# Opening of the expert stages with four units ahead of the first down product

## The reference, cut to what matters

```python
def hier_moe(xn, w_group, b_group, w_expert, b_expert, w_gate, w_up, w_down):   # xn = rms_norm(h, ln_ffn)
    g_prob = softmax(xt @ w_group + b_group); g_w, g_idx = top_k(g_prob, 1)      # 4 groups
    e_prob = softmax(of the 8 experts of that group); e_w, e_idx = top_k(e_prob, 2)
    comb = g_w * e_w / sum(e_w);  cw = comb at the chosen experts, 0 elsewhere     # [tokens, 32]
    hid = silu(xt @ w_gate[e]) * (xt @ w_up[e])                                   # all 32 experts
    y = sum over e of (hid * cw[:, e]) @ w_down[e]
```

## Time and profile before

| | |
|---|---|
| median of 3 runs | 4208.21 us (4208.19 to 4209.12) |
| profiled execution | 4201.7 us, span 4199.9 us |
| TensorE matmul busy | 3884.0 us, 92% of the span |
| VectorE busy | 2685.7 us, 64% |
| ScalarE busy | 1813.2 us, 43% |
| GpSimd busy | 1456.4 us, 35% |
| mean TensorE clock granted | 0.922 |
| DMA | 664.37 MB, mean 158 GB/s |

### The profile page before, as it was taken

How to read it: one execution, slowest core, us unless ns; L and a number is a source line. 1 busy time by engine, 2 the same in 40 slices (tenths; PEclk the granted TensorE clock), 3 DMA queues, 4 the chain that set the end, 5 groups by cost and what they waited for, 6 DMA issues and landing times.

```text
span 4199.9 us, 69359 instructions
## 1 busy us (share of the span) xinstructions
PE 3884.0 (92%) x28940; PEld 3543.8 (84%) x28940; DVE 2685.7 (64%) x4863; ACT 1813.2 (43%) x3080; POOL 1456.4 (35%) x842
## 2 busy tenths in 40 slices
PE   7998998989989898979999989989999999999899
PEld 6658997679979867769999859989869998867699
DVE  4446776577777775567777867777657644665543
ACT  3233444334454442234545635444444444432343
POOL 2003443044434430034444423434314444320143
PEclk9759998699989999989999999999969999979899
DMA  5104662156646420027575415657516644210143
GB/s 207 56 16 177 259 263 103 59 192 261 254 167 264 179 95 13 1 106 271 226 271 197 151 51 200 267 211 271 190 53 241 264 168 158 96 41 1 45 168 115
DMA packets 63687, 664.37 MB, mean 158 GB/s; under 512 B 7056, under 2 KB 7568, under 8 KB 7952
## 3 DMA queue, kind: packets, MB, share of 16 engines
q1 hardware_dynamic: 63376, 659.94, 41.8%
HBM read 658.86 MB, written 1.05 MB: 157 GB/s over the span
## 4 chain that ended last, share of the span: by engine, by line
PE 79%; DVE 14%; ACT 4%; issue 1%; POOL 1%; DMA 0%; SPq 0%; DVEq 0%; ACTq 0%; POOLq 0%
PE pb L275 76%; PE pb L282 3%; DVE wp L228 2%; DVE wk L240 2%; DVE wk L228 2%; ACT wp L266 2%; DVE sq L240 1%; DVE ada_acc L240 1%; DVE hT L240 1%; ACT wk L266 1%; DVE sq L228 1%; DVE hx L240 0%; DVE hx L228 0%; POOL sq L228 0%; POOL wp L228 0%
## 5 line engine op out<-in xcount | busy, mean ns | idle before, releaser
L275 PE MATMUL pb<-hx,wp 128*128 128x256 f32 x15744 | 1995.8, 288 | 106.7 <-DVE hx L228 51.8
L275 PEld LDWEIGHTS pb<-hx,wp 128*128 128x128 f32 x15744 | 1956.4, 196 | 128.6 <-issue 106.6
L228 POOL TENSOR_TENSOR wp<-ring,wp 128x512 fp32r<-128x512 f32 (+1 forms) x596 | 1250.3, 2114 | 2005.8 <-ACT wp L266 2005.8
L266 ACT ACTIVATE wp<-ring 128x1024 fp32r<-128x1024 f32 x936 | 941.2, 1046 | 258.1 <-PE pb L275 250.9
L228 DVE TENSOR_TENSOR wp<-ring,wp 128x1024 fp32r<-128x1024 f32 (+1 forms) x670 | 796.8, 1206 | 359.3 <-ACT wp L266 355.3
L275 PE MATMUL pb<-ex,wp 128*128 128x256 f32 x5856 | 756.7, 287 | 19.4 <-DVE ex L228 19.4
L275 PEld LDWEIGHTS pb<-ex,wp 128*128 128x128 f32 x5856 | 728.9, 194 | 20.6 <-issue 18.0
L240 DVE SCALAR_TENSOR_TENSOR ada_acc<-ring,cact,ada_acc 128x384 f32<-128x384 f32 x576 | 529.8, 983 | 60.4 <-ACT ada_acc L266 60.2
L275 PE MATMUL pb<-wk 128*128 128x128 f32 (+8 forms) x3136 | 488.4, 327 | 16.8 <-ACT wk L266 7.7
L275 PEld LDWEIGHTS pb<-wk 128*128 128x128 f32 (+4 forms) x3136 | 339.8, 190 | 160.3 <-issue 96.6
L228 DVE TENSOR_TENSOR sq<-sq,pb 128x256 f32<-128x256 f32 (+1 forms) x360 | 161.4, 448 | 323.6 <-ACT sq L266 276.3
(11 more groups left out here) (179 smaller groups left out, 2821.2 us busy)
## 6 DMA issues: line engine op xcount, KB each, us to landing
ring<-weights SPq DMA_DIRECT2D x385, 1536.0 KB, 6.7
ring<-weights SPq DMA_DIRECT2D x41, 1024.0 KB, 4.8
ring<-weights SPq DMA_DIRECT2D x4, 512.0 KB, 10.2
cst<-consts SPq DMA_DIRECT2D x1, 2032.0 KB, 11.8
ring<-weights SPq DMA_DIRECT2D x1, 1280.0 KB, 5.5
prm<-params SPq DMA_DIRECT2D x1, 1258.0 KB, 7.4
ring<-weights SPq DMA_DIRECT2D x1, 1152.0 KB, 4.9
xT<-xT_in SPq DMA_DIRECT2D x1, 1024.0 KB, 4.8
```

Of the source, the lines that this page charges most:

```text
L228: return self.real.tensor_tensor(out, a, b, op) if self.real else Uncounted()
L266: return self.real.activation(out, a, func, bias=bias, scale=scale, accum_out=accum)
L275: return self.real.matmul(out, l, r, start=start, stop=stop, skip_group_check=skip)
```

## The change

Stage 1 and stage 4 open with `first` = 3. Down pieces of the opening are cast and halved one unit later (units 0, 1) or after the choice (units 2, 3: `g.rest`), so the early pieces of the stage are two, not three. 1/rms is made as in the other stages (`norm_root_act` L704, `norm_dve` L713: Ln, Exp and Identity on ScalarE, three instructions on VectorE), squares come in pairs (five products). The activation's low halves are made straight from the residual by one `stt`; the router's weights are multiplied by the gain once (`wrg`, over `hT`) and the logits come from `X3`. The two transposes of the choice stand in the middle of units 1 and 3. The gates of units 0 to 2, the up products, the weights and the halves are named in an order of their own, and the side job of unit 2 goes to unit 5 (`u == first + 2 > 2`).

```diff
+        loaded = []
+
+        def part_of(u, j):
+            c = loaded[u]
+            p = piece(c.dst[:, j * PIECE:(j + 1) * PIECE], c, next(slot) % NPIECE, ("v", "vg", "g")[j], after)
+            g.pieces[u].append(p)
+            return p
+
+        def fetch():
+            u = len(loaded)
+            loaded.append(chunk(128, 3072, lambda I: unit(I, u)))
             g.pieces.append([])
-            for j, by in enumerate(bys):
-                g.pieces[u].append(piece(c.dst[:, j * PIECE:(j + 1) * PIECE], c, next(slot) % NPIECE, by, after))
-
-        fetch(("v", "vg", "g"))
+            g.split.append([part_of(u, 0), part_of(u, 1)])
+            if u > first or first == 0:
+                g.split[u].append(part_of(u, 2))
+            elif u == first:
+                g.rest += [part_of(u - 1, 2), part_of(u, 2)]
+            elif u:
+                g.split[u].append(part_of(u - 1, 2))
...
-            if u % 2 and pend is not None:
+                fetch()
...
-            if u % 2 == 0 and u >= first:
+                fetch()
+            if u >= first and (u % 2 == 0 or u == first + 2 > 2):
                 pend = g.ada[u] = plan_ada()
...
+                if b == 0 and u in middle:
+                    middle[u]()
...
-            if u >= g.first:
+            if u == g.first > 0:
+                for n in range(u):
+                    spread(n)
+                for n in range(u):
+                    down(n)
+                spread(u)
+            elif u >= g.first:
                 if cw is not None:
-                    for n in range(0 if u == g.first else u, u + 1):
-                        spread(n)
-                for n in range(0, u) if u == g.first else [u - 1]:
-                    down(n)
+                    spread(u)
+                if u:
+                    down(u - 1)
...
     def glu_pool(e, g):
         for u in range(1, g.units):
-            split_lo_g(e, g.pieces[u])
+            split_lo_g(e, g.split[u])
+            if u == g.first:
+                e.wait_ge(*x_lo[g.st, "hid", u - 1])
+                split_lo_g(e, g.rest)
...
-                bk.hold(e, 0, (st, "var"), (v_step, (st, "var")))
+                bk.hold(e, 0, (st, "mean"), (a_out, (st, "minus half")))
+                for k in (0, 2, 4, 6, 7):
+                    e.wait_ge(*g_step[(st, "pair", k + 1) if k < 6 else (st, "square", k)])
+                    ins = e.mm(bank(st, "mean")[:, 0:T], ones[:, 0:128], Q3[:, k, :], k == 0, k == KD - 1)
+                ins.then_inc(*summed.up((st, "mean")))
+                bk.hold(e, 1, (st, "lg"), (v_out, (st, "lg")))
+                e.wait_ge(*v_step[st, "router"])
                 for k in range(KD):
-                    e.wait_ge(*g_step[st, "square", k])
-                    ins = e.mm(bank(st, "var")[:, 0:T], ones[:, 0:128], Q3[:, k, :], k == 0, k == KD - 1)
-                ins.then_inc(*summed.up((st, "var")))
-                bk.hold(e, 1, (st, "lg"), (v_out, (st, "lg")))
-                for k in range(KD):
-                    ins = e.mm(bank(st, "lg")[0:36, 0:T], wr[:, k, :], H3[:, k, :], k == 0, k == KD - 1)
+                    ins = e.mm(bank(st, "lg")[0:36, 0:T], wrg[:, k, :], X3[:, k, :], k == 0, k == KD - 1)
                 ins.then_inc(*summed.up((st, "lg")))
...
-            glu_pe(e, G_, ready, (norm_and_logits, logits_by_token, weights_by_expert), both_cw[:, :])
+            glu_pe(e, G_, ready, (norm_and_logits,), both_cw[:, :], {1: logits_by_token, 3: weights_by_expert})
...
-                e.ts(H3[:, k, :], X3[:, k, :], gain(k), None, ALU.mult).then_inc(*v_step.up((st, "h", k)))
-                e.wait_ge(*v_step[st, "h", k])
+                e.wait_ge(*x_new[st - 1, k])
                 e.wait_ge(*x_hi[st, "h", k])
-                e.tt(Hl[:, k, :], H3[:, k, :], Hh[:, k, :], ALU.subtract).then_inc(*x_lo.up((st, "h", k)))
-
-            def norm_and_logits():
-                split_lo_v(e, G_.pieces[1])
-                e.wait_ge(*summed[st, "var"])
-                e.wait_ge(*v_step.last)
-                e.ts(nv[:, :], bank(st, "var")[:, 0:T], 1.0 / D, 1e-6, ALU.mult, ALU.add).then_inc(*v_step.up((st, "var")))
-                newton(e, rsb[:, :], nv[:, :], nm[:, :], nt[:, :], (st, "rs"))
-                e.wait_ge(*v_step[st, "rs"])
+                e.stt(Hl[:, k, :], X3[:, k, :], gain(k), Hh[:, k, :], ALU.mult, ALU.subtract).then_inc(
+                    *x_lo.up((st, "h", k)))
+            e.tt(wrg, wr, pc(f"ln_ffn{l}", 0, 8).unsqueeze(2).to_broadcast([128, 8, 36]), ALU.mult).then_inc(
+                *v_step.up((st, "router")))
+
+            def norm_and_logits(gate, up, weigh, low):
+                split_lo_v(e, G_.split[1])
+                norm_dve(e, st)
+                split_lo_v(e, G_.split[2])
...
-            def logits_by_token():
+            def choice(gate, up, weigh, low):
                 e.wait_ge(*turned[st, "lgt"])
                 e.copy(lg, bank(st, "lgt")[:, 0:72].rearrange("p (b n) -> p b n", b=2)).then_inc(*v_out.up((st, "lgt")))
-                split_lo_v(e, G_.pieces[2])
                 choose(e)
-
-            def weights_by_expert():
+                split_lo_v(e, G_.split[3])
+
+            def gates(gate, up, weigh, low):
+                for u in range(3):
+                    gate(u)
+
+            def weighed(gate, up, weigh, low):
                 e.wait_ge(*turned[st, "cwt"])
                 e.tt(cwT, bank(st, "cwt")[0:32, 0:T], rsb[0:32, :], ALU.mult).then_inc(*v_out.up((st, "cwT")))
+                up(0)
                 e.wait_ge(*x_hi[st, "cwT"])
                 e.tt(both_cw[32:64, :], cwT, both_cw[0:32, :], ALU.subtract).then_inc(*x_lo.up((st, "cwT")))
+                up(1)
+                up(2)
+                for u in range(3):
+                    weigh(u)
+                    if u:
+                        low(u - 1)
+                low(2)
+                split_lo_v(e, G_.split[4])
+                gate(3)
+                up(3)
+                weigh(3)
+                low(3)
...
+            e.tables("natural_log_exp_and_others")
...
-                split_hi(e, G_.pieces[1])
-
-            def logits_by_token():
-                split_hi(e, G_.pieces[2])
+            def three_units(silu, high):
+                split_hi(e, G_.split[1])
+                split_hi(e, G_.split[2])
+                norm_root_act(e, st)
+                split_hi(e, G_.split[3])
+
+            def choice(silu, high):
                 for name, a in (("ge", ge), ("e2", e2)):
                     e.wait_ge(*v_step[st, name])
                     e.act(a, a, ACT.Exp).then_inc(*a_step.up((st, name)))
-
-            def weights_by_expert():
+                split_hi(e, G_.rest)
+
+            def gates(silu, high):
+                silu(0)
+
+            def weighed(silu, high):
                 e.wait_ge(*v_out[st, "cwT"])
                 e.act(both_cw[0:32, :], cwT, ACT.Copy).then_inc(*x_hi.up((st, "cwT")))
-
-            glu_act(e, G_, (norm_and_logits, logits_by_token, weights_by_expert), True)
+                silu(1)
+                silu(2)
+                for u in range(3):
+                    high(u)
+                split_hi(e, G_.split[4])
+                silu(3)
+                high(3)
...
+                if k in (1, 3, 5):
+                    e.wait_ge(*g_step[st, "square", k])
+                    e.tt(Q3[:, k - 1, :], Q3[:, k - 1, :], Q3[:, k, :], ALU.add).then_inc(*g_step.up((st, "pair", k)))
```

More of the change, by code:

```diff
@@ L869, in part, with glu_pe @@
         return [a[:, c:c + 128] for a in halves]
-    def glu_pe(e, g, ready, hooks=(), cw=None):
+    def glu_pe(e, g, ready, hooks=(), cw=None, middle={}):
         st = g.st
@@ L948, in hidden @@
             e.wait_ge(*v_out[st, "cw" if cw else "glu", u])
-            e.act(eh[n], sg[n], ACT.Copy).then_inc(*x_hi.up((st, "hid", u)))
+            e.act(eh[u % 3], sg[u % 3], ACT.Copy).then_inc(*x_hi.up((st, "hid", u)))
         for u in range(g.units):
             if u < len(hooks):
[L953 to L957, removed]
+                hooks[u](silu, high)
+                continue
@@ L958, in glu_act @@
+            split_hi(e, g.split[u + 1] if u + 1 < g.units else early(st + 1))
             if g.ada.get(u) is not None:
                 ada_act(e, g.ada[u], st)
[L960 to L964, removed]
+            silu(u)
+            high(u)
     def glu_dve(e, g, finish, hooks=(), cw=False):
         st = g.st
[L969 to L974, removed]
-                e.wait_ge(*v_step[st, "rs"])
[L976 to L986, removed]
@@ new lines, in gate, with up, weigh @@
+        def gate(u):
+            e.wait_ge(*product[st, "glu", u])
+            e.wait_ge(*v_step[st, "scale"])
+            if u >= 3:
+                e.wait_ge(*product[st, "down", u - 3, 7])
+            e.tt(sg[u % 3], bank(st, "glu", u)[:, 0:T], rsb[:, :], ALU.mult).then_inc(*v_step.up((st, "gate", u)))
+        def up(u):
+            e.wait_ge(*a_out[st, "silu", u])
```

(21 more changed lines are left out.)

31 lines of the change are left out of this document (15 added, 16 removed).

## The result

The changed kernel takes 4186.11 us (median of 4 runs, 4185.66 to 4188.58) against 4208.2 before: ratio 0.9949, interval [0.9933, 0.9965]. That is 22.1 us less, where 28.3 less were forecast; the time lies in the range. In a second job the difference between the medians was 15.2 (4192.34 against 4207.55).

A forecast was written before the change was run, and what follows sets the result against it. TensorE, busy for 92% of the span, was taken as the bound, with the gain ahead of the first down product. Stage 1's 12.9 us and stage 4's 15.4, together 28.3, off the median 4208.2 gave 4179.9; range 4170 to 4193.

The forecast's parts named there:

- The opening: Stages 1 and 4, up to the first down product: it comes earlier, for a gain of 13.2 and 15.9 us.
- the hole in unit 1: Middle of unit 1: TensorE waits for the scaled logits and their bias, a new stall of 2.5 us.
- the turns at the port: VectorE steps with both operands in SBUF wait for GpSimd's running piece; the root steps alternate with five pieces, 8.7 us.
- Spread 3: Behind the third down product: TensorE waits for unit 3's bank, a stall of 1.7 us, between 0 and 1.7 plus 2.4.
- The clock: Clock at 1.00 throughout; downs 0 and 1 at full clock win 1.4 us in stage 1 and 1.2 in stage 4.
- The modulation steps: Units 4, 5 and 6 have one each; VectorE falls 2.7 us behind under some 5.9 of cover, cost 0.
- From T+11 on no hole until the stage's end: T is the start of down 0; from 11 us after it, no hole was expected until the stage's end.
- The sum: Both expert stages: 12.9 us in stage 1 and 15.4 in stage 4, together 28.3, giving 4179.9; chance 0.52.
- Rival (a): No turn taking at the port, so both stalls vanish: gain 36.7 us, 4171.5; chance 0.22.
- (b): Openings: VectorE loses one more whole GpSimd piece each, four stalls lower the clock: gain 16.9 us, 4191.3; chance 0.19.
- (c): Unit 0 isn't freed, 3.8 us lost per stage, plus larger waits and lower clock: gain 8.3, 4199.9; chance 0.04.
- (d), the ring: Weight transfers in one order come over 12 us later, TensorE waits in units 4 to 8: slower, 4217; chance 0.03.

The follow-up runs named there:

- the small step: Changed kernel with the six VectorE products of unit 5's modulation step cut from 384 columns to 16 in both expert stages; stage ends at 307.64 / 307.80 us.
- the five traces named above: Changed kernel (4186.11 us), its repeat (4192.34), with unit 5's modulation step cut, with GpSimd held back at two places (ratio 0.9946), with GpSimd's new order alone (ends 308.17 / 308.19).

## Why the prediction was right, and where its sum was not

- **The opening.** The holes came where they were forecast, and the first down product 1.9 sooner: 36.0 from the cast forecast, 34.11 measured. The largest part is the hole in unit 1, 1.36 and not 2.5: the turns at the port came in the forecast order, but GpSimd's five pieces ended 14.6 from the cast and not 15.6, so the third root step ended at 14.9 instead of 16.0, and the logits' bias was ready at 17.3 instead of 18.6. The sums took 2.32 (2.5), and some 0.7 more was won behind the transposes. The forecast gain was 13.2 and 15.9, measured 15.1 and 17.8.
- **Spread 3.** A hole of 1.21 (1.7), by the mechanism given: it went when 4b's half was put ahead of 3-down. Rival (a), no turn taking, is refuted by the root steps of 2.47 and 1.40 with pieces running and 0.42 without. The Trainium skill, SBUF — State Buffer, section "Who interferes with whom", says that the order of issue decides who blocks; by that rule the same instruction costs either figure, and the two traces agree: the step of 2.47 was issued behind a running piece, the one of 0.42 met none.
- **The clock.** 1.00 throughout the opening, as forecast. Behind it, it wasn't: in stage 4 it fell behind the waits of 1.52 and 0.60 and cost 1.5. At the stage's end the last down product took 4.95, 4.61 and 5.42 in traces where the wait was 5.06, 3.38 and 4.61; before, with waits of 3.36 and 3.38, it took 3.10 in stage 1 and 4.31 in stage 4. So at one length of wait it came out both ways, and why is not settled here.
- **The modulation steps: the term that was mis-sized.** The forecast priced three in a row at 0, from 10.0 busy us of VectorE a unit: 2.7 behind, under a cover of 5.9. What counts is VectorE's round, 11.97. Of this 10.4 to 10.5 is busy time (the forecast took 13.64 busy us in a window of 17.5 for two units, which last 18.17 and have 14.27), and 1.5 are waits for ScalarE (Silu, high half, casts). Three such rounds are 8.6 behind, more than the cover. From unit 4 to unit 31 the changed kernel took 4.4 and 5.9 more than the kernel before, and at the end 2.4 and 0.3 more: 12.9, of which 1.4 are the matmuls of a step that stood ahead of unit 4 before. "From T+11 on no hole until the stage's end" was wrong. Taking the third step away gave 6.1 and 5.5 back.
- **The sum.** The 11.5 that are left are, but for rounding, the 7.9 by which the forecast missed (28.3 less 20.4) and the 3.7 by which both openings together were better than forecast. That these two errors had opposite signs is luck: with the opening as forecast, the gain would have been some 16.7 by these numbers, near the upper end of the range.
- **Rivals (b) to (d).** (b), 16.9, lies nearer to the 20.4 than the forecast does, but not by its mechanism: the openings had neither a further whole piece to wait for nor the low clock. The low clock came behind the openings. (c): unit 0 took 5.99. (d), the ring: no wait of TensorE in units 4 to 8 has a transfer as its cause, and with the small step, all transfers unchanged, they shrank with VectorE's round.

## What to carry to other kernels

An engine's busy time per unit says little of whether it keeps up: take its round, from one instruction to the same one a unit later, with the waits in between, before a side job is placed in consecutive units. Compare it with the round of the engine that sets the pace too: the difference, here some 0.15 in 18.2, is all that it can catch up with, and at that rate a lag of 2.9 in unit 9 was still 1.4 in unit 31. An engine that shares a port must be given the places where its pieces do no harm; holding it back from one chain puts it beside the next. A gain at the head of a stage is only kept if the other engines come as much sooner; here 1.2 of 2.9 was lost again in the last wait.

## What the runs showed of the hardware beyond the forecast

A GpSimd piece stops even the smallest VectorE instructions: a product of 8 columns took 1.15 us and a pair of scans over 4 columns 1.29 beside it, against 0.17 and 0.24 in the changed kernel's choice, which had GpSimd idle. VectorE's root steps and GpSimd's pieces took turns, one instruction each. The clock fell without one long wait: two of at most 1.52 and 0.60, with six matmuls of one column between them, stood ahead of it in seven of ten stages (the five traces named above), and in three it held. Two executions of the changed kernel differ by some 5 us ahead of stage 1 (336.35 and 331.57).
